# Score products of the latents' attention, issued sorted by the number of rows of their operands within a head pair

## The chip, the core and the metric

The kernel runs on one core of one Trainium2 chip. The metric is the device time of one execution in microseconds (us); lower is better. TensorE (PE in the profile) does the matrix products, VectorE (DVE) and ScalarE (ACT) the elementwise work, GpSimd (POOL) some of it, and SyncE (SP) issues the loads of weights.

## What is computed

The reference is two networks in a row on 512 tokens of width 1024. The first block mixes a gated delta rule with dilated attention and ends in a layer with product-key experts. The second block has two layers. Each mixes gated linear attention, neighborhood attention and sliding-window attention over 512 latents and 256 context tokens, and then runs a gated feed-forward network. The change touches the latents' neighborhood and window attention only, whose scores are

```python
# neighborhood attention, 6 heads of width 64: keys near each query, and the context's keys
s_loc = jnp.einsum('brnqhd,brnkchd->bhrnqkc', q_blk, k_blk).astype(jnp.float32) * scale + bias
s_ctx = jnp.einsum('brnqhd,blhd->bhrnql', q_blk, kc).astype(jnp.float32) * scale
# sliding window, 6 query heads on 2 key heads: 3 blocks of 128 keys, and the context's keys
s_loc = jnp.einsum('bnqhgd,bnkhd->bhgnqk', qb, kb).astype(jnp.float32) * scale
s_ctx = jnp.einsum('bnqhgd,blhd->bhgnql', qb, kc).astype(jnp.float32) * scale
```

each followed by a softmax over both parts and the product with the values.

## The kernel before

**Precision.** Every float32 operand of a large product is split into an upper part, rounded to the format that TensorE multiplies in one pass, and a lower part, the rest. A product is the sum of upper x upper, lower x upper and upper x lower. In the weight products that is three matmuls (lines 463, 465 and 474) of 128 rows each. In the attention a head has only 64 features, so two of the three parts fit into one matmul: the upper half of an operand's 128 rows holds one part and the lower half the other. One score product of a head is therefore a pair of matmuls: a *whole* one with operands of 128 rows (queries `nqd` or `sqs`, keys `nks`, `rks`, `skd` or `rskd`), and a *half* one with operands of 64 rows (`nql` with `nks` or `rks` in the neighborhood, `sqs` with `skl` or `rskl` in the window). The half one adds to the columns that the whole one has just written. The half matmuls of head 0 of a pair have their operands in rows 0 to 63, those of head 1 in rows 64 to 127.

**Items.** The attention's work is cut into items: one item is a pair of heads and one tile of 128 queries. A layer has 12 neighborhood items and 12 window items. `cuts[p]` lists for head p the pieces of columns of PSUM and the operands of the whole and the half matmul of each. Neighborhood items, and window items at both ends of the sequence, have 512 columns of scores per head. Head 0 fills one bank of PSUM and head 1 the next, in four pieces and eight matmuls. Window items in the middle of the sequence have 640 columns per head, so that the two heads meet within a bank: five pieces, ten matmuls, three banks. The keys are the moving operand (256 columns in most pieces), the queries the stationary one, loaded anew for each matmul.

**Order.** Each item is a small program per engine (`attend`). TensorE writes the scores and gives the semaphore marks "half" after head 0 and "scores" after head 1. VectorE (line 2308) reads them with the bias, finds the smallest value and stores them in SBUF (`NS`, `SS`). ScalarE (line 2274) takes the exponential, VectorE and ScalarE divide (lines 2331, 2334 and 2281), TensorE turns the weights (line 2247), ScalarE and VectorE copy them back (2287, 2340), TensorE multiplies with the values (line 2255, operands of 128 rows and 64 columns), and VectorE copies the result out (2344). A planner that runs when the kernel is built interleaves these items with weight products and puts all of it into one fixed order per engine. It counts the yields of each program and not its matmuls. Each engine then runs its own list in order, and only semaphores tie them.

The loop that issues the scores before the change is, for each head,

```python
for c0, c1, parts in it.cuts[p]:
    ...
    for k, (q, key) in enumerate(parts):
        ins = t.x.matmul(sp[:, c0:c1], q, key, start=k == 0, stop=k == len(parts) - 1)
```

Of the kernel before, what the change touches and what calls it, by code (L numbers as in the profile page):

```python
# [331 lines left out]
def program(nc, io):  # L332
# [52 lines left out]
    def hold(t, b, *by):  # L385
        for flag in freed.get(b, ()):
            t.wait_ge(*flag)
        freed[b] = by
        return bank[b]
# [1784 lines left out]
    def next_item(e, lane):  # L2174

        k = e.state[lane.name] = e.state.get(lane.name, -1) + 1
        if laying(e):
            left = lists[lane.m.name, lane.items]
            for j in (k, k + 1):
                if (lane.name, j) not in assigned:  # L2180
                    assigned[lane.name, j] = left.pop(0) if left else None
        return assigned[lane.name, k]

    def pick(t, lane, step, it):

        def left():
            return [g[:it.count] for g in lane.groups if not busy & set(g[:it.count])]
        if laying(t):
            while not left():
                yield Until(left)  # L2190
            group_of[step, it.key] = min(left(), key=lambda g: max(free_at.get(b, 0.0) for b in g))
# [17 lines left out]
    def attend(lane):  # L2209
        S, m = lane.S, lane.m  # L2210

        def tensor(t):
            while it := next_item(t, lane):
                n = it.n
                yield When(("operands", m.name, it.out))
                if out_event(it):
                    yield When(out_event(it))
                yield from pick(t, lane, "scores", it)
                for b in group_of["scores", it.key]:
                    hold(t, b, ("attend_v", it.key, "least", 1) if it.bias is not None else ("attend_a", it.key, "exp", 1))  # L2220
                note(t, "scores", it, it.count == 1, 3.5)
                sp = banks_of("scores", it)
                operands_tensor(t, it)
                shared = {c0 // 512 for c0, _, _ in it.cuts[0]}
                for p in range(2):
                    if p and it.count == 1:
                        yield 0.5
                    for c0, c1, parts in it.cuts[p]:
                        if p and c0 // 512 in shared:
                            t.wait_ge("attend_t", it.key, "half")  # L2230
                        for k, (q, key) in enumerate(parts):
                            ins = t.x.matmul(sp[:, c0:c1], q, key, start=k == 0, stop=k == len(parts) - 1)
                    ins.then_inc(*t.gives("attend_t", it.key, "scores" if p else "half"))
                note(t, "scores", it, False, 3.5)
                yield Mark(("swept", it.key))
                yield 4.0
                yield from pick(t, lane, "turn", it)
                note(t, "turn", it, True)
                sp = banks_of("turn", it)
                for b in group_of["turn", it.key]:  # L2240
                    hold(t, b, ("attend_v", it.key, "out"))
                for k in range(it.count):
                    t.wait_ge("attend_v", it.key, "weights")
                    if cells(it, k).stop > n:
                        t.wait_ge("attend_a", it.key, "weights")
                    for b in range(4 * k, cells(it, k).stop // 128):
                        ins = t.x.transpose(sp[:, 128 * b:128 * b + 128], S[:, 128 * b:128 * b + 128], ident)
                    ins.then_inc(*t.gives("attend_t", it.key, "turn", k))
                yield 1.0
                values_tensor(t, it)  # L2250
                for k in range(it.count):
                    t.wait_ge(*turned(it, k))
                for j in range(n // 128):
                    for p in range(2):
                        ins = t.x.matmul(sp[hs[p], 0:128], it.vals[p][j], S[:, n * p + 128 * j:n * p + 128 * j + 128],
                                         start=j == 0, stop=j == n // 128 - 1)
                ins.then_inc(*t.gives("attend_t", it.key, "out"))
                note(t, "turn", it, False, 0.6)
                if laying(t):
                    attended[it.m.name, it.out] = attended.get((it.m.name, it.out), 0) + 1  # L2260
                    if attended[it.m.name, it.out] == m.NT:
                        yield Mark(("attended", m.name, it.out))
                yield 0.2
# [128 lines left out]
    def out_event(it):  # L2392

        if not it.m.lat:
            return f"split {it.m.name} {it.out - 3}" if it.out >= 3 else None
        if it.out >= 4:
            return f"split {it.m.name} {it.out - 4}"
        return f"values {it.m.name} {it.out - 1}" if it.out else None
# [1588 lines left out]
```

## Time and profile before

| | |
|---|---|
| time, median of 3 runs | 4315.93 us (4309.71 to 4316.92) |
| time of the profiled execution | 4310.04 us |
| its span on the core | 4308.2 us |
| TensorE busy | 3970.9 us, 92% of the span |
| VectorE busy | 2391.3 us, 56% |
| ScalarE busy | 1690.4 us, 39% |
| mean granted clock of TensorE | 0.946 |

The span is the time from the core's first to its last instruction; 1.8 us of the execution lie outside it. A matmul's record has a start and a duration that includes the way through the array, so that records overlap; what a matmul costs in a row of others is the distance from its start to the next one's start. The granted clock is 1.0 at 2.4 GHz and 0.5 at 1.2 GHz.

### The profile page before, as it was taken

The numbers are of one execution on the slowest core, as the hardware profiler recorded it, in microseconds if no ns is written. First come the engines' busy times: TensorE is split into PE (matmuls) and PEld (weight loads), VectorE is DVE, ScalarE is ACT, GpSimd is POOL, SyncE is SP. The second block draws the span as 40 slices with busy tenths as digits, with TensorE's granted clock in tenths as the row PEclk, the third lists the DMA queues.
The fourth block names the chain that finished last, engine by engine and source line by source line (L and its number), as shares of the span: only waits on it lengthen the run. The fifth ranks groups of instructions, "written<-read, shape, count | busy, mean of one in ns | idle before, by whom it ended". The sixth has DMA issues, their size and how long they took to land. (4 is left out here: it accounts for less than half of the span.)

```text
span 4308.2 us, 57393 instructions
## 1 busy us (share of the span) xinstructions
PE 3970.9 (92%) x23037; PEld 3390.5 (79%) x23037; DVE 2391.3 (56%) x4212; ACT 1690.4 (39%) x2807; POOL 731.4 (17%) x580
## 2 busy tenths in 40 slices
PE   7899998988898779999999999888899998899998
PEld 4678876776798779999999998666688776567887
DVE  4444324455788758777777776545533345545333
ACT  3422333343356773333333334334432233444222
POOL 0012000252214423223222322000000010101000
PEclk8999999998998889999999999987899999869999
DMA  5311234432344458888888884211133431101322
GB/s 200 116 45 38 65 106 149 170 100 76 104 160 161 144 199 303 274 286 278 282 287 273 288 276 147 79 49 36 67 126 120 137 122 52 61 20 61 98 96 79
DMA packets 209193, 617.30 MB, mean 143 GB/s; under 512 B 18464, under 2 KB 68640, under 8 KB 205088
## 3 DMA queue, kind: packets, MB, share of 16 engines
q1 hardware_dynamic: 168352, 465.76, 33.2%
q0 software_dynamic: 40576, 147.87, 9.8%
q8 instruction: 183, 3.00, 0.3%
q14 instruction: 82, 0.67, 0.1%
HBM read 583.67 MB, written 29.88 MB: 142 GB/s over the span
## 5 line engine op out<-in xcount | busy, mean ns | idle before, releaser
L463 PE MATMUL ps<-hhi,whi 128*128 128x512 f32 (+1 forms) x2824 | 1100.1, 390 | 29.4 <-ACT whi L421 19.2
L429 DVE TENSOR_TENSOR wlo<-raw,whi 128x1024 fp32r<-128x1024 f32 x576 | 714.1, 1240 | 715.4 <-ACT whi L421 715.1
L465 PE MATMUL ps<-hlo,whi 128*128 128x512 f32 (+1 forms) x2824 | 1064.8, 377 | 0.3 <-DVE hlo L2440 0.2
L421 ACT ACTIVATE whi<-raw 128x1024 fp32r<-128x1024 f32 x660 | 694.1, 1053 | 664.3 <-PE ps L474 507.8
L474 PE MATMUL ps<-hhi,wlo 128*128 128x512 f32 (+1 forms) x2824 | 671.3, 376 | 0.0
L463 PEld LDWEIGHTS ps<-hhi,whi 128*128 128x128 f32 x2824 | 543.4, 192 | 135.6 <-issue 47.5
L465 PEld LDWEIGHTS ps<-hlo,whi 128*128 128x128 f32 x2824 | 543.7, 193 | 74.0 <-issue 7.2
L474 PEld LDWEIGHTS ps<-hhi,wlo 128*128 128x128 f32 x2824 | 514.7, 190 | 74.4 <-issue 5.7
L463 PE MATMUL ps<-ag_hi,whi 128*128 128x384 f32 x1024 | 342.2, 334 | 0.0
L465 PE MATMUL ps<-ag_lo,whi 128*128 128x384 f32 x1024 | 342.1, 334 | 0.0
L429 POOL TENSOR_TENSOR wlo<-raw,whi 128x1024 fp32r<-128x1024 f32 x85 | 206.4, 2436 | 322.5 <-ACT whi L421 322.1
L3310 POOL DMA_INDIRECT fetched<-peer_u_rows,rows x128 | 149.0, 1164 | 389.0 <-DVE ract L3268 344.5
L3310 POOL DMA_INDIRECT fetched<-peer_v_rows,rows x128 | 149.5, 1168 | 363.1 <-DVE xtok L3282 338.7
L3195 ACT ACTIVATE uact<-ps 128x384 f32<-128x384 f32 x128 | 62.9, 492 | 373.4 <-PE ps L474 373.4
L474 PE MATMUL ps<-ag_hi,wlo 128*128 128x384 f32 x1024 | 198.1, 334 | 0.0
L463 PE MATMUL ps<-hchi,whi 128*128 128x256 f32 x672 | 180.0, 301 | 17.1 <-ACT whi L421 8.1
L463 PEld LDWEIGHTS ps<-ag_hi,whi 128*128 128x128 f32 x1024 | 192.3, 188 | 0.0
L465 PEld LDWEIGHTS ps<-ag_lo,whi 128*128 128x128 f32 x1024 | 192.2, 188 | 0.0
L474 PEld LDWEIGHTS ps<-ag_hi,wlo 128*128 128x128 f32 x1024 | 179.3, 187 | 0.0
L465 PE MATMUL ps<-hclo,whi 128*128 128x256 f32 x672 | 173.3, 291 | 0.0
L3268 DVE CUSTOM_DVE_ANT_0 fetched<-fetched,xtok 128x1024 f32<-128x1024 f32 x128 | 156.0, 1219 | 12.3 <-DMA fetched<-peer_u_rows,rows 12.3
L3282 DVE SCALAR_TENSOR_TENSOR xtok<-fetched,ract,xtok 128x1024 f32<-128x1024 f32 x127 | 162.4, 1279 | 0.0
(629 smaller groups left out, 6189.9 us busy)
## 6 DMA issues: line engine op xcount, KB each, us to landing
raw<-w_in SPq DMA_DIRECT2D x151, 512.0 KB, 3.6
raw<-peer_u SPq DMA_DIRECT2D x128, 512.0 KB, 4.7
raw<-peer_v SPq DMA_DIRECT2D x128, 512.0 KB, 4.2
raw<-w_mod SPq DMA_DIRECT2D x96, 512.0 KB, 4.2
raw<-w_gate SPq DMA_DIRECT2D x66, 512.0 KB, 3.5
raw<-w_up SPq DMA_DIRECT2D x66, 512.0 KB, 3.5
raw<-w_down SPq DMA_DIRECT2D x66, 512.0 KB, 3.5
gate_dram<-stage SPq DMA_DIRECT2D x24, 1024.0 KB, 4.6
```

What stands on the lines that cost most here:

```text
L421: a.x.activation(whi[n % NW][:], raw[i % NRAW][:], ACT.Copy, bias=0.0, scale=1.0).then_inc(*a.gives("hi", i))
L429: e.x.tensor_tensor(wlo[n % NW][:], raw[i % NRAW][:], whi[n % NW][:].bitcast(F32), ALU.subtract).then_inc(*e.gives(*lo_sig(i)))
L463: t.x.matmul(o, w, p.hi, start=grp.opens and k == 0, stop=False)
L465: t.x.matmul(o, w, p.lo, start=False, stop=False)
L474: ins = t.x.matmul(o, lo[:, 128 * (starts[gi] + k):128 * (starts[gi] + k) + 128], p.hi, start=False, stop=grp.closes and k == len(grp.pair ...
L3195: a.x.activation(uact[j % 2][:], held(("out", "peer_u", j))[:, 0:TD], ACT.Gelu_apprx_tanh, bias=0.0, scale=1.0).then_inc(*a.gives("peer_a" ...
L3268: v.x.tensor_tensor_reduce(c[:], c[:], xtok[:], 1.0, 0.0, ALU.mult, ALU.add, ract[:, i:i + 1]).then_inc(*v.gives("expert_v", "dot", i))
L3282: v.x.scalar_tensor_tensor(xtok[:], c[:], ract[:, i:i + 1], xtok[:], ALU.mult, ALU.add).then_inc(*v.gives("expert_v", "sum", i))
L3310: g.x.indirect_dma_start(fetched[i % NF][:], None, io["peer_v_rows" if i >= 128 else "peer_u_rows"], bass.IndirectOffsetOnAxis(ap=rows[:, ...
```

## The change

Within each head of an item all whole matmuls are now issued first and then all half ones, and in head 1 of an item whose heads share no bank it is the other way round, so that the half ones of both heads stand together. `shared` is now the set of banks that both heads write; only matmuls into those wait for "half". In a bank that a head writes in several pieces, only the first matmul has `start` and only the last has `stop`. The context's own attention has one matmul per piece, and its order stays as it was.

```diff
-                shared = {c0 // 512 for c0, _, _ in it.cuts[0]}
+                shared = {c0 // 512 for c0, _, _ in it.cuts[0]} & {c0 // 512 for c0, _, _ in it.cuts[1]}
                 for p in range(2):
                     if p and it.count == 1:
                         yield 0.5
-                    for c0, c1, parts in it.cuts[p]:
-                        if p and c0 // 512 in shared:
+                    pieces = sorted(it.cuts[p], key=lambda x: x[0] // 512 in shared) if p else it.cuts[p]
+                    whole, halves = [[(c0, c1, *parts[k]) for c0, c1, parts in pieces if k < len(parts)] for k in range(2)]
+                    row = halves + whole if p and not shared else whole + halves
+                    banks = [c0 // 512 for c0, _, _, _ in row]
+                    for k, (c0, c1, q, key) in enumerate(row):
+                        if p and banks[k] in shared:
                             t.wait_ge("attend_t", it.key, "half")
-                        for k, (q, key) in enumerate(parts):
-                            ins = t.x.matmul(sp[:, c0:c1], q, key, start=k == 0, stop=k == len(parts) - 1)
+                        ins = t.x.matmul(sp[:, c0:c1], q, key, start=banks[k] not in banks[:k], stop=banks[k] not in banks[k + 1:])
                     ins.then_inc(*t.gives("attend_t", it.key, "scores" if p else "half"))
```

The score matmuls stand at line 2232 before and at line 2235 after the change. On VectorE, ScalarE, GpSimd and SyncE the order of the instructions is the same before and after; on TensorE nothing moves but the score matmuls within their items.

The first place is the first neighborhood item of the first layer on TensorE. Before the change its eight matmuls stand so (rows with `nqd` are whole ones, rows with `nql` half ones; the first four belong to head 0):

```order
L2232 MATMUL ps<-l_nks_386,l_nqd_384 128x256
L2232 MATMUL ps<-l_nks_386,l_nql_385 128x256
L2232 MATMUL ps<-l_rks_387,l_nqd_384 128x256
L2232 MATMUL ps<-l_rks_387,l_nql_385 128x256
L2232 MATMUL ps<-l_rks_387,l_nqd_384 128x256
L2232 MATMUL ps<-l_rks_387,l_nql_385 128x256
L2232 MATMUL ps<-l_nks_386,l_nqd_384 128x256
L2232 MATMUL ps<-l_nks_386,l_nql_385 128x256
```

After the change the same item reads as follows; the row marked x2 is the last half matmul of head 0 and the first one of head 1.

```order
L2235 MATMUL ps<-l_nks_386,l_nqd_384 128x256
L2235 MATMUL ps<-l_rks_387,l_nqd_384 128x256
L2235 MATMUL ps<-l_nks_386,l_nql_385 128x256
L2235 MATMUL ps<-l_rks_387,l_nql_385 128x256 x2
L2235 MATMUL ps<-l_nks_386,l_nql_385 128x256
L2235 MATMUL ps<-l_rks_387,l_nqd_384 128x256
L2235 MATMUL ps<-l_nks_386,l_nqd_384 128x256
```

Two whole matmuls now open the item, four half ones stand in its middle, and two whole ones close it.

The second place is a window item in the middle of the sequence, whose heads share a bank. Before the change its ten matmuls on TensorE alternate (rows with `skd` and `rskd` are whole ones, with `skl` and `rskl` half ones; the first six belong to head 0):

```order
L2232 MATMUL ps<-l_skd,l_sqs_398 128x128
L2232 MATMUL ps<-l_skl,l_sqs_398 128x128
L2232 MATMUL ps<-l_skd,l_sqs_398 128x256
L2232 MATMUL ps<-l_skl,l_sqs_398 128x256
L2232 MATMUL ps<-l_rskd,l_sqs_398 128x256
L2232 MATMUL ps<-l_rskl,l_sqs_398 128x256
L2232 MATMUL ps<-l_rskd,l_sqs_398 128x256
L2232 MATMUL ps<-l_rskl,l_sqs_398 128x256
L2232 MATMUL ps<-l_skd,l_sqs_398 128x384
L2232 MATMUL ps<-l_skl,l_sqs_398 128x384
```

After the change, on TensorE, the same item:

```order
L2235 MATMUL ps<-l_skd,l_sqs_398 128x128
L2235 MATMUL ps<-l_skd,l_sqs_398 128x256
L2235 MATMUL ps<-l_rskd,l_sqs_398 128x256
L2235 MATMUL ps<-l_skl,l_sqs_398 128x128
L2235 MATMUL ps<-l_skl,l_sqs_398 128x256
L2235 MATMUL ps<-l_rskl,l_sqs_398 128x256
L2235 MATMUL ps<-l_rskd,l_sqs_398 128x256
L2235 MATMUL ps<-l_skd,l_sqs_398 128x384
L2235 MATMUL ps<-l_rskl,l_sqs_398 128x256
L2235 MATMUL ps<-l_skl,l_sqs_398 128x384
```

Each head is now a group of whole matmuls and a group of half ones. The wait for "half" stands ahead of the matmul with 384 columns of `skd` in both orders; one matmul now lies between it and head 0's last one, where two did before.

## Rows read from the trace of the kernel before

**Rows 1.** The page: busy time by engine, and TensorE's granted clock in 40 slices.

```profile
PE 3970.9 (92%) x23037; PEld 3390.5 (79%) x23037; DVE 2391.3 (56%) x4212; ACT 1690.4 (39%) x2807; POOL 731.4 (17%) x580
...
PEclk8999999998998889999999999987899999869999
```

**Rows 2.** Windows: stretch, length, busy us by engine, granted clock, DMA share, GB/s.

```profile
2838.00:3086.00 248.00, 214.45 (x1044) 149.78 (x1044) 126.56 (x305) 112.06 (x221) 13.33 (x16) 0.78 0.11 35
```

**Rows 3.** Timeline of TensorE, a neighborhood item at full clock: start, us, instruction.

```profile
2922.26 0.38 PE L2232 MATMUL ps<-l_nks,l_nqd 128*128 128x256 f32 x1
...
2924.76 0.50 PE L474 MATMUL ps<-hhi,wlo 128*128 128x512 f32 x1
```

**Rows 4.** Timeline of TensorE, a neighborhood item at half clock, and what follows.

```profile
2958.65 0.58 PE L2232 MATMUL ps<-l_nks,l_nqd 128*128 128x256 f32 x1 [1.45 <-DVE l_o L2344]
...
2962.73 0.47 PE L2255 MATMUL ps<-l_NS,l_nvtok 128*64 128x128 f32 x1
```

**Rows 5.** Timeline of TensorE, weight products of 256 columns, full and half clock.

```profile
851.02 0.28 PE L463 MATMUL ps<-hchi,whi 128*128 128x256 f32 x1
851.14 0.28 PE L465 MATMUL ps<-hclo,whi 128*128 128x256 f32 x1
...
886.48 0.41 PE L463 MATMUL ps<-hchi,whi 128*128 128x256 f32 x1
886.69 0.41 PE L465 MATMUL ps<-hclo,whi 128*128 128x256 f32 x1
```

**Rows 6.** Timeline of TensorE, context scores of 64 rows between weight products.

```profile
987.26 0.40 PE L463 MATMUL ps<-hhi,whi 128*128 128x512 f32 x1
987.50 0.40 PE L465 MATMUL ps<-hlo,whi 128*128 128x512 f32 x1
987.82 1.56 PE L2232 MATMUL ps<-c_res,c_nq 64*128 64x256 f32 x6
989.31 0.51 PE L463 MATMUL ps<-hhi,whi 128*128 128x512 f32 x1
```

**Rows 7.** Windows of line 2232 alone (PE, PEld, granted clock, DMA), half-clock stretches.

```profile
2838.60:2862.30 23.70, 8.28 (x16) 4.58 (x16) 0.57 0.13 45
...
2951.20:3005.70 54.50, 30.65 (x60) 17.21 (x60) 0.50 0.00 1
...
3029.70:3050.10 20.40, 13.45 (x26) 7.42 (x26) 0.50 0.00 0
...
3657.80:3678.10 20.30, 6.60 (x13) 3.54 (x13) 0.58 0.15 52
...
3883.00:3896.60 13.60, 9.08 (x18) 5.19 (x18) 0.50 0.00 0
```

**Rows 8.** Timeline of TensorE, context scores of one item and of two items together.

```profile
1047.68 0.70 PE L2232 MATMUL ps<-c_res,c_sq 64*128 64x256 f32 x2
...
1050.45 0.70 PE L2232 MATMUL ps<-c_res,c_sq 64*128 64x256 f32 x4
```

**Rows 9.** Timeline of VectorE after the first layer's first item.

```profile
2843.84 0.69 DVE L2308 CUSTOM_DVE_ANT_0 l_NS<-ps,l_NB 128x512 f32<-128x512 f32 x1
...
2851.85 0.69 DVE L2066 TENSOR_TENSOR l_tmp<-ps,l_C 128x512 f32<-128x512 f32 x1 [5.55 <-ACT l_C L1983]
```

**Rows 10.** Timeline at the end of the first layer's window items, VectorE and TensorE.

```profile
3073.79 0.88 DVE L2308 CUSTOM_DVE_ANT_0 l_SS<-ps,l_swm,nsink 128x640 f32<-128x640 f32 x1
...
3077.57 0.73 DVE L2308 CUSTOM_DVE_ANT_0 l_SS<-ps,l_swm,nsink 128x512 f32<-128x512 f32 x1
...
3082.74 0.29 PE L2255 MATMUL ps<-l_SS,l_res 128*64 128x128 f32 x1 [2.38 <-ACT l_SS L2287]
```

**Rows 11.** Timeline of TensorE, a window item that waits for its banks.

```profile
3029.67 0.58 PE L2232 MATMUL ps<-l_skd,l_sqs 128*128 128x256 f32 x1 [1.79 <-DVE l_st L2308]
```

**Rows 12.** Windows, all engines: neighborhood items among weight products; five window items.

```profile
2903.00:2944.00 41.00, 41.00 (x241) 28.25 (x240) 20.82 (x54) 17.80 (x35) 6.21 (x7) 1.00 0.25 82
...
2981.00:3003.00 22.00, 22.00 (x45) 12.30 (x43) 10.51 (x37) 9.15 (x23) 0.00 (x0) 0.50 0.00 0
```

## The prediction

> **What bounds the kernel now.** I read the page first: TensorE is busy 92% of the span [rows 1], so what matters is what its time is made of. Its clock is high in most slices and dips deepest in two places, slices 27 to 29 and 35 to 36 of 108 us each, and that is where the latents' attention of the two layers lies. The window over the first of them shows 248 us with TensorE busy for 214, VectorE for 127 and ScalarE for 112, at a mean clock of 0.78 [rows 2]; the second layer's window reads the same to within 1 us. TensorE is the bound there too, but with 248 - 214 = 34 us of waits per layer, so a matmul saved does not always shorten the stretch.
>
> Then I read the timeline, by distances from start to start. At full clock the eight score matmuls of an item take from 2922.26 to 2924.76, which is 0.3125 us each for 256 columns [rows 3]. At half clock they take from 2958.65 to 2962.73, 0.51 us each [rows 4]. A weight product of the same 256 columns costs 0.12 us at full clock and 0.21 us (0.213 over a longer row) at half clock [rows 5]. Those also add one matmul after the other into the same columns, so that the accumulation is not what costs. What differs is that the score matmuls alternate between operands of 128 and of 64 rows. The context's scores, all of 64 rows, isolate it: six of them, with neighbours of 128 rows at the two ends only, take from 987.82 to 989.31, 0.25 us each and less than the 0.3125 of the alternation, while the weight product of 512 columns just before them takes 0.32 us instead of the 0.24 of the one before it [rows 6]. The cost sits at the switch between the two forms, not in the form.
>
> **The change, step by step.**
>
> *Price of a switch.* 0.3125 - 0.12 = 0.1925 us at full clock, 0.51 - 0.213 = 0.297 us at half clock [rows 3 to 5]. Each matmul pays one switch now, since each has a neighbour of the other form on both sides.
>
> *How many go.* An item of eight matmuls has eight switches (its last leads back to a form of 128 rows) and keeps two; one of ten has ten and keeps four. Both lose six, and 48 items in two layers lose 288 of 408.
>
> *At which clock.* The half-clock stretches of the first layer hold 16 + 60 + 26 = 102 of its 204 score matmuls; those of the second, five stretches of which the first and last are shown, hold 105 [rows 7]. So 207 of 408 are at half clock, and of the switches removed 146 at 0.297 = 43.4 us and 142 at 0.1925 = 27.3 us. Together 70.7 us of TensorE.
>
> *Half matmuls of two heads side by side.* In 36 of the items the last half matmul of head 0 (rows 0 to 63, first bank) is now followed by the first of head 1 (rows 64 to 127, next bank). Four context matmuls of two items, in other rows and banks, took the same 0.70 us as two [rows 8]: such neighbours run at once. That hides one matmul per item, 0.107 us at full and 0.213 at half clock (256 columns at 2.4 and 1.2 GHz, just under the distances in [rows 5]), 18 items of each: 5.8 us more. From below it could be nothing.
>
> *Switches that stay after all.* Four half-clock items are followed directly by products with the values, which are of a third form (128 rows, 64 columns) [rows 4]; there a closing whole matmul has to switch too. 4 x 0.3 = 1.2 us back.
>
> *The wait for "half".* In the 12 items of ten matmuls the wait now comes one matmul after head 0's last one. Its record lasts 0.58 us at half clock [rows 4], and by then only about 0.51 + 0.21 us have passed before the waiting matmul could start. What is behind it on TensorE is the rest of the item, and its weight load can't be made early. I take 0.12 us each, 1.5 us, between nothing and a whole record (12 x 0.58 = 7 us). The other waits are unchanged, and "half" comes earlier for VectorE in the other items.
>
> *What the gain is lost to.* TensorE's list is fixed, so the question at each wait is whether what it waits for moves with the scores. Mostly it does: before 3029.67 TensorE waits 1.79 us for VectorE's two reads of scores that TensorE has just finished [rows 11], and this pair shifts as a whole. In three places it doesn't.
> First, each layer's first item: VectorE starts its read at 2843.84 with no idle time before, being busy with other operands until then, and TensorE later waits for line 2066, which hangs on ScalarE's list [rows 9]. The item's whole saving, 6 x 0.297 + 0.21 = 2.0 us at half clock, is lost, twice: 3.8 us with the second one partly at full clock.
> Second, each layer's last two window items: VectorE takes one item every 3.8 us (3073.79 to 3077.57) without idle time, and TensorE waits 2.38 us for the end of this chain [rows 10]. In the first layer that swallows the saving of the last two items, 12 x 0.1925 + 0.11 = 2.4 us. In the second the two are at half clock and save 3.8 us; TensorE reaches the same place later there, and I take 2.4 us of them as lost.
> Third, the item at 3029.67 and its twin: VectorE is still in the softmax of the item before when the scores are ready, about 0.5 us each.
> Together 3.8 + 4.8 + 1.0 = 9.6 us. The DMAs are at 0.11 of their time here [rows 2] and don't matter. The order of the other engines is the same, so nothing else moves.
>
> *Sum.* 70.7 + 5.8 - 1.2 - 1.5 - 9.6 = 64.2 us. On top, what is left of each stretch should run somewhat more often at full clock, since the same columns come in less time: the last short dip of the first layer (3074 to 3077) may vanish, and the clock may return a little earlier behind the window items. I allow 3 us. The profiled execution took 4310.04 us; 4310.0 - 67 = 4243. It is at the low end of the runs of before (4309.7 to 4316.9), so I put the time at 4244.
>
> *A rule against the change.* Were weight loads not hidden between two matmuls on the same rows, grouping would pay a load at each of the junctions it makes. The weight products show no such thing: same rows each time, and 0.12 us for 256 columns [rows 5], against 0.107 for the columns alone.
> The Trainium skill, "TensorE: Matmul & The Clock Gate", section "The mechanism" of its part on packing small matmuls, says that a weight load overlaps running matmuls only when the row groups differ; in another section it also allows it for a load into the background weight buffer. By the first sentence alone, each of the 288 new junctions would cost 128 columns at 1.2 GHz, an estimate of 0.107 us or 31 us in all, and the time would be about 4275. The trace sides with the second.
>
> **The rivals.**
>
> *More of it is absorbed (0.10).* VectorE and ScalarE need about 3.8 us per window item [rows 10], and five such items stand in a row, 22 us of TensorE [rows 12]. If this chain sets the pace wherever items stand close, the saving of the roughly 20 window items near others shrinks from 1.8 to about 0.6 us each, 24 us less: 4268. Against it: VectorE is busy only 10.5 of those 22 us [rows 12], and banks are freed after its reads, which come ahead of the rest of the chain.
>
> *The clock comes back (0.14).* In [rows 12] TensorE's records cover all 22 us and the clock is still 0.50; at 2922 the same alternation, between weight products, runs at 1.0 [rows 3]. If the closer order brings the window items to full clock, the half-clock items cost 0.9 us less again (8 x 0.51 - 6 x 0.297 = 2.3 against 8 x 0.3125 - 6 x 0.1925 = 1.35), and the other matmuls of these stretches gain as well. With 207 of 408 matmuls that is 24 items, 23 us; for the rest, what the stretches of [rows 7] hold beside the scores, I put 12 us; VectorE's chain takes back about half of the 35: 4226.
>
> The skill's same page, section "What's actually happening", has the clock follow how busy TensorE is. By that rule the stretch in [rows 12] would already be at full clock if busy meant covered by records, so the trace asks for another measure, and the denser order can only help; it leans to this rival.
>
> *The switch isn't what costs (0.03).* If the 0.19 us came with each half matmul wherever it stands, the change would move nothing: 4311 to 4316. Against it stand the context's scores, half matmuls in form, at 0.25 us each with two switches among six [rows 6], and four of them in the time of two [rows 8].
>
> *Slower (0.02).* The neighborhood items at full clock stand among weight products; from 2903 to 2944 TensorE has no wait at all and the clock is 1.0 [rows 12]. If TensorE, done sooner, waited more and its clock fell to half there, these 41 us of work would take up to 41 us more in each layer: 4246 + 82 = 4328. It decides once more than 64 us are lost so. For it: the clock is already down where items stand without weight products between them. Against it: nothing but dead time is taken out, and what replaces it is the next matmul, not a wait.
>
> **How the numbers follow.** My forecast has 0.71, with a range of its own from 4230 to 4262: the unknown terms are the side-by-side term (0 to 5.8), the wait for "half" (0 to 7), the losses (5 to 20) and the clock (0 to 15). The range for 8 in 10 reaches partly to both neighbours: 4222 to 4266. A measurement of this kernel tells 0.2%, some 9 us, from no change. Faster by more than that: 0.71 + 0.10 + 0.14 and a small part of the switch rival's failure to be complete, 0.95. Within it 0.03, slower 0.02.
>
> **What the profile after would show.** Within an item at full clock two whole matmuls start about 0.12 us apart, and an item of eight takes about 1.25 us at full and 2.1 at half clock instead of 2.50 and 4.08; the last half matmul of head 0 and the first of head 1 start within some nanoseconds. The stretch from the first score to the last value product shrinks by about 32 us in each layer, and everything ahead of 2838 is unchanged. The wait at 3082.74 grows to nearly 5 us. I would be wrong in the switch's price if whole matmuls follow at 0.2 us or more, in the losses if TensorE's waits per layer grow by much more than 5 us, and in the clock if the stretch around the five window items is at 1.0.

## The result, and the profile after

| | before | after |
|---|---|---|
| time, median | 4316.43 us (4309.71 to 4321.0, 4 runs) | 4267.24 us (4263.78 to 4270.94, 4 runs) |
| profiled execution, span | 4310.04, 4308.2 us | 4268.82, 4267.0 us |
| TensorE busy | 3970.9 us | 3885.8 us |
| mean granted clock | 0.946 | 0.952 |

The changed kernel is faster: the ratio is 0.9889 with a 95% interval of 0.9876 to 0.9901, or 49 us. The forecast was 4244 with a range up to 4266; the measured median lies 1 us above that range. The direction was right, and the gain two thirds of what was expected.

The page of the changed kernel, busy time by engine and TensorE's clock in 40 slices, against [rows 1]:

```profile
PE 3885.8 (91%) x23037; PEld 3355.6 (79%) x23037; DVE 2390.1 (56%) x4212; ACT 1686.0 (40%) x2807; POOL 728.7 (17%) x580
...
PEclk8999999999999899999999999988899999879999
```

TensorE's busy time fell by 85 us, that of the other engines hardly. The span fell by 41, so about half of what TensorE saved did not reach it. The windows over the two layers' stretches of the changed kernel (stretch, length, busy us by engine, granted clock, DMA share, GB/s), against [rows 2]:

```profile
2843.00:3070.00 227.00, 176.86 (x1082) 135.47 (x1083) 126.27 (x307) 109.73 (x221) 13.30 (x16) 0.81 0.13 39
3637.00:3862.00 225.00, 174.42 (x1082) 134.32 (x1083) 125.63 (x305) 109.02 (x220) 13.29 (x16) 0.82 0.13 39
```

TensorE now stands idle for 50 of 227 us where it was idle for 34 of 248. The timeline of TensorE of the changed kernel, a neighborhood item at full clock, against [rows 3]:

```profile
2921.59 0.38 PE L2235 MATMUL ps<-l_nks,l_nqd 128*128 128x256 f32 x1
2921.81 0.28 PE L2235 MATMUL ps<-l_rks,l_nqd 128*128 128x256 f32 x1
2922.02 0.38 PE L2235 MATMUL ps<-l_nks,l_nql 64*128 64x256 f32 x1
2922.03 0.49 PE L2235 MATMUL ps<-l_rks,l_nql 64*128 64x256 f32 x2
2922.25 0.28 PE L2235 MATMUL ps<-l_nks,l_nql 64*128 64x256 f32 x1
2922.46 0.39 PE L2235 MATMUL ps<-l_rks,l_nqd 128*128 128x256 f32 x1
2922.68 0.28 PE L2235 MATMUL ps<-l_nks,l_nqd 128*128 128x256 f32 x1
2922.80 1.10 PE L474 MATMUL ps<-hhi,wlo 128*128 128x512 f32 x4
```

The eight matmuls take 2922.80 - 2921.59 = 1.21 us instead of 2.50. Read the distances of the closing group: from the last half matmul to the next whole one 2922.25 to 2922.46, 0.21 us; from this whole one to the next 0.22 us; from the last whole one to the weight product 0.12 us. So a switch costs 0.09 us ahead of it and 0.10 us behind it, 0.19 together, as the prediction had it in one piece. The four half matmuls start in two pairs: two at 2922.02 and 2922.03, two within 0.01 us of each other at 2922.25 (the row marked x2 holds the second of the first pair and the first of the second). Which of them make a pair shows in an item of the changed kernel in which both heads take the keys in the same order, so that its list has `l_skl`, `l_rskl` of head 0 and then `l_skl`, `l_rskl` of head 1:

```profile
3015.32 0.39 PE L2235 MATMUL ps<-l_skl,l_sqs 64*128 64x256 f32 x2
3015.55 0.28 PE L2235 MATMUL ps<-l_rskl,l_sqs 64*128 64x256 f32 x2
```

The two with `l_skl` start together and, 0.22 us later, the two with `l_rskl`. So each half matmul of head 0 runs beside its counterpart of head 1, and head 1's first one starts ahead of head 0's second, against the order of the list.

TensorE, an item at half clock, and the wait ahead of it, against [rows 4] and, for the wait, [rows 9]:

```profile
2858.45 0.58 PE L2235 MATMUL ps<-l_nks,l_nqd 128*128 128x256 f32 x1 [7.84 <-DVE l_tmp L2066]
...
2860.49 0.84 PE L2540 MATMUL ps<-cst,l_nvT 128*128 128x128 f32 x3
```

That is 2.04 us instead of 4.08. **Where the time went** follows from the distances between the starts of TensorE's matmuls, split at each layer's first window item (what stands in brackets in the timeline is the wait, the rest is work; the first start and the last value product bound the stretch):

| part | before: us, of them waits | after |
|---|---|---|
| layer 0, neighborhood part | 141.5, 25.0 | 128.5, 32.3 |
| layer 0, window part | 108.2, 7.2 | 97.2, 17.0 |
| layer 1, neighborhood part | 140.3, 26.0 | 127.2, 33.3 |
| layer 1, window part | 107.0, 4.8 | 97.0, 16.9 |
| sum | 497.0, 63.0 | 449.9, 99.5 |

Work fell from 434.0 to 350.4, by 83.6 us; the score matmuls alone fell from 166.9 to 83.1. Waits grew by 36.5, of them 21.9 in the window parts. Net 47.1 us. (The profiled span shows 41 and not 47 because this execution reached the first score at 2843.86 instead of 2839.38. The code ahead is the same, and the profiled executions of the experiments reach it between 2839.5 and 2845.1.)

**The waits in the window part.** TensorE of the changed kernel, some of its rows in the run of five window items that [rows 12] showed without a wait, and behind it:

```profile
2972.33 0.27 PE L2235 MATMUL ps<-l_skd,l_sqs 128*128 128x256 f32 x1
...
2978.42 0.50 PE L2235 MATMUL ps<-l_skd,l_sqs 128*128 128x128 f32 x2 [1.64 <-DVE l_st L2311]
...
2981.93 0.58 PE L2235 MATMUL ps<-l_skd,l_sqs 128*128 128x256 f32 x1 [0.69 <-DVE l_st L2311]
...
2989.12 1.31 PE L2250 MATMUL ps<-cst,l_SS 128*128 128x128 f32 x10 [1.16 <-DVE l_st L2311]
```

Three items, 26 matmuls, start between 2972.33 and 2976.49; then TensorE waits for VectorE's reads of scores, which free the banks. VectorE's timeline of the changed kernel shows why these reads are late:

```profile
2973.30 0.75 DVE L2311 CUSTOM_DVE_ANT_0 l_SS<-ps,l_swm,nsink 128x512 f32<-128x512 f32 x1
...
2974.76 0.16 DVE L2327 TENSOR_TENSOR l_st<-l_st,nsink 128x2 f32<-128x2 f32 x1
2975.81 0.16 DVE L2330 TENSOR_TENSOR l_st<-l_st 128x2 f32<-128x2 f32 x1 [0.88 <-ACT l_st L2282]
2976.01 0.17 DVE L2334 RECIPROCAL l_st<-l_st 128x1 f32<-128x1 f32 x1
2976.21 0.49 DVE L2337 TENSOR_SCALAR l_SS<-l_SS,l_st 128x512 f32<-128x512 f32 x1
2976.61 0.16 DVE L2334 RECIPROCAL l_st<-l_st 128x1 f32<-128x1 f32 x1
2976.68 0.87 DVE L2311 CUSTOM_DVE_ANT_0 l_SS<-ps,l_swm,nsink 128x640 f32<-128x640 f32 x1
...
2980.46 0.73 DVE L2311 CUSTOM_DVE_ANT_0 l_SS<-ps,l_swm,nsink 128x512 f32<-128x512 f32 x1
```

On VectorE's fixed list the read of the next item's scores stands behind the whole softmax of this one, with a wait of 0.88 us for ScalarE's exponentials in the middle. VectorE takes one item per 3.38 us (2973.30 to 2976.68) or 3.78 us (to 2980.46), in turn for 512 and 640 columns. TensorE's score matmuls now take 1.2 us for eight and 2.0 for ten at full clock (2.0 and 3.4 at half clock); with 4.08 us for eight it was the slower of the two in this run before (22 us for five items, 4.4 each). Now VectorE's list is.

**The waits in the neighborhood part.** In the first layer the wait of [rows 9]'s line 2066 grew from 5.07 to 7.84 us, another from 5.77 to 6.77, and three are new. The first of these, on ScalarE and on TensorE of the changed kernel:

```profile
2909.00 0.72 ACT L2284 ACTIVATE l_NS<-l_NS,l_st 128x512 f32<-128x512 f32 x1 [0.23 <-DVE l_st L2334]
2909.63 0.58 ACT L1776 ACTIVATE l_sq<-ps 128x512 f32<-128x512 f32 x1
```

```profile
2910.35 1.18 PE L2621 MATMUL ps<-l_sq,c 128*128 128x512 f32 x2 [1.53 <-ACT l_sq L1776]
2926.50 1.10 PE L2621 MATMUL ps<-l_sk,c 128*128 128x512 f32 x2 [1.50 <-ACT l_sk L1776]
2941.10 0.63 PE L2627 MATMUL ps<-cst,l_svT 128*128 128x128 f32 x4 [1.53 <-ACT l_svT L1776]
```

ScalarE copies the fresh projection `l_sq` out of PSUM only after the scaling that ends an item's softmax on its list. TensorE, whose scores between the projection and its next use got shorter, now comes 1.5 us too soon. The stretch that [rows 12] had without a wait and at 1.00 holds such waits now and is at 0.93, while the window items' run is at full clock at its start. Windows of the changed kernel:

```profile
2903.00:2944.00 41.00, 36.44 (x246) 27.81 (x242) 22.77 (x60) 19.53 (x41) 6.91 (x8) 0.93 0.27 87
...
2972.00:2977.00 5.00, 4.77 (x29) 3.29 (x27) 3.40 (x11) 2.23 (x7) 0.00 (x0) 1.00 0.00 0
```

### The profile page after: what moved, and what is told of

Its sections match the earlier page's. It is cut to its first block and busy times, and to the rows that moved or that the text cites. A ratio compares the mean times of both kernels' runs of the same rounds, so it can differ in the third digit from the quotient of the medians.

```text
span 4267.0 us, 57393 instructions
## 1 busy us (share of the span) xinstructions
PE 3885.8 (91%) x23037; PEld 3355.6 (79%) x23037; DVE 2390.1 (56%) x4212; ACT 1686.0 (40%) x2807; POOL 728.7 (17%) x580
## 5 line engine op out<-in xcount | busy, mean ns | idle before, releaser
L465 PEld LDWEIGHTS ps<-hlo,whi 128*128 128x128 f32 x2824 | 543.3, 192 | 73.8 <-issue 7.0
```

Source lines behind the costliest of these rows:

```text
L465: t.x.matmul(o, w, p.lo, start=False, stop=False)
```

## The experiments

Times are medians with the lowest and highest run. The kernel before was run with each group: 4314.72 us (4311.64 to 4322.63) with the first four, 4316.78 (4310.76 to 4324.96) with the next four, 4316.12 (4310.99 to 4322.34) with the three after these, and 4313.6 (4312.45 to 4319.25) with the last. A ratio is to that one. Parts, waits and work are counted as in the table above.

**1 and 2. One kind of item each.** The new order only where the condition holds, the old loop elsewhere; the second has `it.out >= 3`.

```diff
+                if it.out < 3:
                     shared = {c0 // 512 for c0, _, _ in it.cuts[0]} & {c0 // 512 for c0, _, _ in it.cuts[1]}
...
+                else:
+                    shared = {c0 // 512 for c0, _, _ in it.cuts[0]}
...
```

Expected of the neighborhood items alone:

> Only the 24 neighborhood items have the new order; the window items alternate as before. Theory A (the gain is the switches removed, less what TensorE then waits longer for VectorE and ScalarE): these items save 8 x 1.29 + 4 x 2.04 = 18.5 us of TensorE per layer, and the waits around them grow by 7.4 us per layer as in the trace of the changed kernel, so about 22 us in all: 4294 us. Rival B (what is lost is lost in the window items alone, whose softmax has the longer chain, and the neighborhood items keep all they save): 37 us, 4279 us.

Expected of the window items alone:

> Only the 24 window items have the new order. Theory A: about 23 us of TensorE per layer saved, a good part of it by the return of the full clock, and about 10 us per layer lost to longer waits: 26 us in all, 4290 us, and the two parts add up to the whole change. Rival B (above): about 12 us, 4304 us. If the parts add to clearly less or more than 49 us, one part's waits hang on the other's.

Measured: 4290.0 us (4284.46 to 4291.46), ratio 0.9934 [0.9917, 0.9950], and 4292.64 us (4290.84 to 4294.17), ratio 0.9944 [0.9928, 0.9961]. The gains, 24.7 and 22.1 us, add up to 46.8, the 49 of the whole within the spread of the runs. Both kinds lose part of their saving by themselves; neither eats the other's.

**3. Without the turn in head 1.**

```diff
-                    row = halves + whole if p and not shared else whole + halves
+                    row = whole + halves
```

> In head 1 of the 36 items of eight matmuls the whole matmuls come first as well, so that these items keep four switches and the half matmuls of the two heads are not neighbours. TensorE needs 2 x 0.19 to 0.3 us more for the switches and 0.11 to 0.21 more for the matmul that is no longer hidden, about 0.65 us per item or 23 us. Theory A: a little over half of it shows, since the waits shrink by the rest: 4280 us. Rival C (VectorE's and ScalarE's chains set the pace wherever items stand, so TensorE's speed no longer matters): within 3 us of the changed kernel, 4267 us. If all of it shows, 4290 us.

Measured: 4270.5 us (4269.49 to 4282.62), ratio 0.990 [0.988, 0.9921]. Of the three forecasts the one of rival C, 4267 within 3 us, came nearest; theory A's 4280 was missed. The items are slower as they should be. TensorE of this kernel, one of them at full clock:

```profile
2921.18 0.39 PE L2235 MATMUL ps<-l_nks,l_nqd 128*128 128x256 f32 x1
...
2922.70 0.28 PE L2235 MATMUL ps<-l_nks,l_nql 64*128 64x256 f32 x1
2922.90 0.50 PE L474 MATMUL ps<-hhi,wlo 128*128 128x512 f32 x1
```

Two more switches and no matmul hidden behind a neighbour: eight starts span 1.52 us (2922.70 - 2921.18), against 1.09 (2922.68 - 2921.59) in the changed kernel. To the product behind it the item takes 1.72 us, where it took 2.50 with the same eight matmuls and four switches more: 0.195 us a switch. Over both layers the score matmuls take 105.1 us instead of 83.1. Yet the stretches grow by only 2.5 us, since 17.1 us of waits go and 2.4 us of other work. A quarter of all that was gained in the scores (22 of 84 us) is worth little here: 3.3 us between the medians, with overlapping runs.

**4. One form only.** The order of before, but every half matmul multiplies the operands of the whole one.

```diff
                         for k, (q, key) in enumerate(parts):
+                            if it.m.lat:
+                                q, key = parts[0]
```

> The order of the kernel before, but each half matmul of the latents multiplies the whole matmul's operands of 128 rows a second time, so all score matmuls have one form and there is no switch at all; the scores are wrong by that. Theory A (a switch between forms costs 0.19 or 0.3 us): the matmuls follow at 0.12 and 0.21 us, an item of eight takes 1.0 us at full clock, less than the 1.21 of the changed kernel, and the time is near that kernel's, 4260 to 4267 us. Rival D (the cost belongs to two matmuls in turn on the same columns, or to the order of the keys): distances stay at 0.31 and 0.51 us and the time at 4316 us.

Measured: 4256.34 us (4250.3 to 4261.66), ratio 0.9856 [0.9837, 0.9874]. TensorE of this kernel, the first item, at half clock:

```profile
2845.07 0.76 PE L2234 MATMUL ps<-l_nks,l_nqd 128*128 128x256 f32 x2 [3.39 <-ACT l_nqd L2585]
2845.63 1.05 PE L2234 MATMUL ps<-l_rks,l_nqd 128*128 128x256 f32 x4
2846.49 0.63 PE L2234 MATMUL ps<-l_nks,l_nqd 128*128 128x256 f32 x2
2846.91 1.05 PE L1920 MATMUL ps<-l_tmp,c 128*128 128x512 f32 x1
```

Eight matmuls in 1.84 us, 0.23 each, with the order and the columns of before and as many weight loads; the time is a little under the forecast. So neither the order of the keys nor two matmuls in turn on the same columns costs anything. This run has no half matmuls at all, so it can't tell a price of the half form from a price of the switch; experiment 3 can, since it keeps all half matmuls and takes away switches. Together they leave the alternation of forms. This kernel has the shortest scores of all, 34.6 us per layer, and the most waits, 54.8.

**5 and 6. A shorter softmax, in the changed kernel and in the one before.** TensorE's list is untouched.

```diff
+                        thin = slice(it.half[0].start, it.half[0].start + 64) if it.m.lat and not isinstance(v.x, Blank) else it.half[0]
-                        v.x.tensor_scalar(S[:, it.half[0]], S[:, it.half[0]], lane.root[:, col[0]], None, ALU.mult).then_inc(
+                        v.x.tensor_scalar(S[:, thin], S[:, thin], lane.root[:, col[0]], None, ALU.mult).then_inc(
...
-                items.append(Item(m, 3 + i, n, w + 256, cuts, vals, bias, nsink[:, 6 * m.l + i:6 * m.l + i + 4:3]))
+                items.append(Item(m, 3 + i, n, w + 256, cuts, vals, bias))
```

(ScalarE's scaling of head 1 in the same way.) Expected of the changed kernel with it:

> The changed kernel with a shorter softmax on VectorE and ScalarE: the weights of both heads are scaled in 64 columns instead of 512 or 640, and the window items leave out the sink (two small operations of VectorE and one of ScalarE, with the wait between the engines); the output is wrong by that. TensorE's list is the same. Theory A: the waits that took 37 us of the change's gain hang on this chain, which gets shorter by about 0.4 us per neighborhood item and 1.5 us per window item, so this kernel gains much more from it than the kernel before does: 4267 - 25 = 4242 us or less. Rival E (the waits hang on something else, such as the loads of bias tables or the evacuation's own time): 4262 us or more.

Expected of the kernel before with it:

> The kernel before with the same shorter softmax. Theory A: TensorE, slower in its scores, mostly hides this chain, so little is gained except where it waits already (5 to 10 us): 4308 us, and the distance to the changed kernel with the short softmax is 60 us or more instead of 49. Rival E: both lose the same, and the distance stays at 49 us.

Measured: 4230.76 us (4228.12 to 4234.82), ratio 0.9799 [0.9783, 0.9815], and 4309.56 us (4306.04 to 4313.39), ratio 0.9985 [0.9975, 0.9994]. The same relief is worth 36 us after the change and 7 before it, and the distance between the two orders grows from 49 to 78.8 us. This is the test of the lost gain: most of it hangs on VectorE's and ScalarE's chain.

**7 and 8. Small matmuls later in the plan.** The planner is made to hold back the rotary products on a fresh projection (line 2621) and the transposes of line 2627 by 1.8 us after ScalarE's copy, and the first neighborhood item by 5 us.

```diff
+    def until(delay):
+        then = plan.now() + delay
+        return Until(lambda: plan.now() >= then)
...
                 yield When(("evac", place_of["proj", (m, *keys[x])], 0))
+                if laying(t):
+                    yield until(1.8)
...
+                if laying(t) and event[1] == "normed":
+                    yield until(5.0)
```

Expected of the changed kernel with it:

> The changed kernel with weight products moved ahead of places where TensorE waits: the planner holds the four small matmuls that read fresh projections of the window attention back by 1.8 us after their evacuation, and the second lane of the neighborhood items by 5 us. No work is added or taken. Theory A: the three waits of 1.53 us per layer and most of the one of 7.8 us are filled, up to 4.6 + 5 us per layer, less what the moved products leave open elsewhere: 4267 - 12 = 4255 us. Rival F (the waits only move on, since the chain on VectorE and ScalarE behind them ends no earlier): 4265 us or more.

Expected of the kernel before with it:

> The same holding back in the kernel before. Theory A: the 1.53 us waits don't exist there, only the one of 5 us before the second neighborhood item can be filled: 4316 - 6 = 4310 us. If it gains as much as the changed kernel does, the waits filled there are not those that the change made.

Measured: 4258.72 us (4256.61 to 4259.91), ratio 0.9862 [0.9845, 0.9878], 8.5 us under the changed kernel. But also 4303.8 us (4301.27 to 4306.04), ratio 0.997 [0.9958, 0.9983], 13 us under the kernel before. The theory's expectation for the second was missed: holding these matmuls back fills waits that the old order had as well. So this version is an improvement of its own, and not evidence of where the gain went.

**9 and 10. The shorter softmax in one kind of item each**, in the changed kernel. The edit is that of 5 with a condition more on `thin`, `it.out < 3` or (shown) `it.out >= 3`; the sink is left out in the second only.

```diff
-                        thin = slice(it.half[0].start, it.half[0].start + 64) if it.m.lat and not isinstance(v.x, Blank) else it.half[0]
+                        thin = slice(it.half[0].start, it.half[0].start + 64) if it.m.lat and it.out >= 3 and not isinstance(v.x, Blank) else it.half[0]
```

Expected with the neighborhood items shortened:

> The changed kernel with a shorter softmax in the neighborhood items only: both engines scale 64 columns of the weights instead of 512 (the rest stays undivided, so the output isn't the reference's). The window items are untouched. With both kinds shortened the time was 4230.8, 36 us below the changed kernel. Theory A, the part of the gain that was lost sits in both kinds, since TensorE's three new waits of 1.5 us per layer stand in the neighborhood part and the grown ones in both: 4250, within 6 us. Rival G, it sits nearly all in the run of window items, where nothing else stands between them: this run stays above 4259.

Expected with the window items shortened:

> The changed kernel with a shorter softmax in the window items only: no sink, and the scaling in 64 columns (the output isn't the reference's). The neighborhood items are untouched. Theory A, the loss is shared: 4248, within 6 us. Rival G, it sits nearly all in the window items: below 4240. The two runs' savings should add up to the 36 us of both together, unless one feeds the other by the clock.

Measured: 4260.09 us (4258.57 to 4261.76), ratio 0.9874 [0.9857, 0.989], and 4237.55 us (4234.66 to 4240.89), ratio 0.982 [0.9804, 0.9836]. The gains of 7.1 and 29.7 us add up to the 36.5 of both. Here the rival is right: this chain limits the window items. VectorE of the second kernel:

```profile
2973.92 0.69 DVE L2314 CUSTOM_DVE_ANT_0 l_SS<-ps,l_swm 128x512 f32<-128x512 f32 x1
...
2976.29 0.80 DVE L2314 CUSTOM_DVE_ANT_0 l_SS<-ps,l_swm 128x640 f32<-128x640 f32 x1
```

An item takes 2.37 us where it took 3.38. Over 24 items that would be 24 us; in the two window parts the waits fell from 33.9 to 15.6 us. TensorE's work in them fell too, from 160.3 to 147.2, in the same list: with fewer waits it ran less at half clock, 30.6 us against 56.3.

In the neighborhood items theory A's 4250 was missed and 4260.09 is where the rival had it. Still the three new waits hang on this chain. ScalarE and TensorE of the first kernel:

```profile
2909.12 0.35 ACT L2285 ACTIVATE l_NS<-l_NS,l_st 128x64 f32<-128x64 f32 x1 [0.23 <-DVE l_st L2335]
...
2910.09 1.10 PE L2623 MATMUL ps<-l_sq,c 128*128 128x512 f32 x2 [1.15 <-ACT l_sq L1776]
```

The scaling ahead of the copy takes 0.35 us instead of 0.72, and the waits are 1.15, 1.14 and 1.15 us instead of 1.53, 1.50 and 1.53. But the wait of 7.34 us for VectorE's copy of the turned weights (line 2258) grew to 8.12. All waits of the two neighborhood parts fell only from 65.6 to 61.7 us, and most of the 7.1 us came as less work of TensorE.

**11. Only the rotary products later**, without the 5 us of the item (the two `until(1.8)` of 7 alone).

> One half of the version that was faster: the planner holds back the small matmuls on fresh projections by 1.8 us after ScalarE's copy, but doesn't hold back the first neighborhood item by 5 us. Theory A, in which the three new waits of 1.5 us per layer for ScalarE's copies are part of what ate the gain and this removes them: 3 x 1.5 x 2 = 9 us, so 4258, as the version with both had. Rival H, the 8.5 us came from the item that was put later: this run stays above 4263.

Measured: 4257.73 us (4254.72 to 4260.41), ratio 0.987 [0.9853, 0.9886]. The 5 us are worth nothing; the whole gain is in the rotary products. It is not quite as expected, though. On TensorE's timeline of this kernel no wait for the copies of `l_sq` and `l_sk` is left between 2895 and 2950, that for `l_svT` now stands ahead of an item, and one of 4.96 us has come, while that of 7.34 us at the products with the values is down to 1.88:

```profile
2924.93 0.39 PE L2239 MATMUL ps<-l_nks,l_nqd 128*128 128x256 f32 x1 [1.21 <-ACT l_svT L1776]
2933.74 1.97 PE L2254 MATMUL ps<-cst,l_NS 128*128 128x128 f32 x8 [4.96 <-DVE l_svtok L2659]
```

The first layer's neighborhood part has 29.0 us of waits, after 32.3, and the part is 3.9 us shorter.

**12. Both reciprocals ahead of the scaling**, in the window items, on top of 11.

```diff
                     v.x.reciprocal(lane.root[:, col[p]], lane.sums[:, col[p]]).then_inc(*v.gives("attend_v", it.key, "root", p))
-                    if p == 0:
+                    if p == (0 if it.sink is None else 1):
                         v.wait_ge("attend_v", it.key, "root", 0)
```

> The version with the later rotary products, and one thing more, in the window items only: VectorE takes both reciprocals before it scales head 0's weights (0.52 us), where it scaled between them, so that ScalarE can scale head 1's weights 0.5 us sooner. TensorE's list is the same as in the version without it; nothing is left out. Theory A, the time of the window items hangs on the chain through their softmax: with no sink and short scaling this chain was some 1.9 us per item shorter (0.16 + 0.19 + 0.16 on the sink, 0.45 and 0.7 in the scaling, and the hops between) and the time fell by 29.7 us; a quarter of that length is about a quarter of the gain, 7 us: 4251, within 4 us. Rival I, only large cuts in this chain reach TensorE since banks are freed by VectorE's reads ahead of it: 4256 to 4260.

Measured: 4250.14 us (4243.89 to 4251.84, 5 runs), ratio 0.9846 [0.9833, 0.986]. ScalarE's timeline of this kernel, the scaling of head 1 in the first window item:

```profile
2967.99 0.72 ACT L2288 ACTIVATE l_SS<-l_SS,l_st 128x512 f32<-128x512 f32 x1 [0.56 <-DVE l_st L2338]
```

VectorE's scaling of head 0 starts at 2967.93, so the two run side by side instead of one after the other. The two window parts take 184.4 us after 189.4. The intervals of 11 and 12 just meet, and they were timed in two sessions; that the second is faster rests on the medians (7.6 us) and on these parts. Why is less clear than the expectation had it: VectorE takes an item of 512 columns per 3.30 us and one of 640 per 3.72, after 3.38 and 3.77 in 11, which over 24 items is some 1.5 of these 5 us. It computes all of the reference and is the fastest such version here: 17 us under the changed kernel, 63.5 under the one before.

## Why the prediction was off

**The price of a switch: right.** 0.19 us at full clock and, at half clock, 0.30 (distances of 0.34 and 0.38 us around a switch against 0.21 without); items of 1.21 and 2.04 us where 1.25 and 2.1 were said. Experiments 3 and 4 together show that it is the alternation. The prediction's own ground for this was weaker than it said: of the six context matmuls of 64 rows in [rows 6], the middle ones, with no switch beside them, start 0.216 us apart and not 0.12. The average of 0.25 hid it, and why they take so long isn't shown. The latents' half matmuls don't: in the item of ten that starts at 2973.44 the middle one of three half ones takes 0.17 us, as the middle one of three whole ones does. The rule weighed against the change, a weight load that can't hide on the same rows, did not show: the two whole matmuls of `l_skd` and `l_rskd` at 2972.33 start 0.11 us apart.
The Trainium skill, "TensorEngine Tiling (Array Packing)", section "Key Properties", says that changing the tiling mode drains TensorE. The trace is in line with it, in that part of each switch is paid ahead of it (0.09 us) and part behind (0.10 us).

**Side by side: right in kind, too small in number.** The prediction had one matmul per item hidden, head 1's first behind head 0's last. Two are, since both half matmuls of head 1 start within 0.01 us of head 0's: the four take two distances (0.22 and 0.21 us) and not three. Within an item of eight the saving of 1.29 us (2.04 at half clock) is near the forecast of 1.26 (2.0) even so. Part of the sixth switch falls on the product behind the item, whose distance went from 0.34 to 0.23 us. Without the turn (experiment 3) the scores take 22.0 us more.

**The wait for "half": over-sized**, 1.5 us forecast and none seen: in the items of ten at half clock and at full clock the waiting matmul starts 0.38 and 0.22 us after the one before, as any first one after a switch does.

**The clock: under-sized in TensorE's work.** 73.8 us were forecast without it and 3 with it; the work fell by 83.6. Of the 408 score matmuls 118 are now at half clock, 204 before. Those 86 are nearly eleven items, and an item costs 0.83 us less at full clock: about 9 us, an estimate from these two figures.

**The step that failed is "What the gain is lost to".** It had 9.6 us in three kinds of places; the waits grew by 36.5. Two of its places were right: the first item (5.07 to 7.84 us; 2.0 were forecast) and the layer's end (2.38 us before; now 1.57, 2.20 and 1.30, which is the forecast of nearly 5). The third was not: the item at 3029.67 and its twin wait 1.79 us in both kernels, and it is the next item's wait that grew, from 0.85 to 2.14. Over both layers the waits of the first two places grew by 13.4 us, where 8.6 were forecast. The other 23 lie elsewhere, 11.5 of them in the run of five window items and just behind it. What it left out is that everything else on VectorE and ScalarE has a place in a list too. I looked for waits that exist and asked how they would grow. I did not ask at which speed of TensorE new ones arise. In the run of window items I set aside the rival that named this with two reasons. One was that VectorE is busy for only 10.5 of 22 us: but its list is held up by waits for ScalarE inside each softmax, so that it can be the bound at half its busy time. The other was that banks are freed by VectorE's reads, ahead of the rest of the chain: true within an item, but the read of the next item stands behind the rest of this one. The rows at hand said 3.8 us per item [rows 10], and my own 2.1 us for an item of eight at half clock, 1.25 at full, would have shown that TensorE outruns it. Experiments 5, 6 and 10 show it from VectorE's side, experiment 3 from TensorE's.
The Trainium skill, "TensorE: Matmul & The Clock Gate", section "Architectural detail: the array is 16× 32×32, not 1× 128×128", says that VectorE's and ScalarE's queues are strictly first in, first out. The rows agree: the read at 2976.68 starts 0.07 us after the start of the reciprocal before it, though the last matmul of its scores started at 2975.14 and lasted 0.33 us.

So the sum was 73.8 + 3 - 9.6 = 67; the runs show 83.6 - 36.5 = 47.1 in the stretches, and 49 in the time. The two misses point in opposite directions, 6.8 us too little work saved and 26.9 us too little waiting, so the total looks better than its terms. "More of it is absorbed" put 4268 and came nearest, with its mechanism; "the clock comes back" happened in part; how much of its 9 us reached the time isn't shown.

**What stays open.** Of the 14.6 us by which the waits of the neighborhood parts grew, experiment 9 shows for the three new ones per layer that they follow the length of ScalarE's softmax. The rest is read from the trace, and a shorter softmax there took only 3.9 us off these waits. The plan change of 7 and 11 gives back 8 to 10 us, but as much or more without the change in order (8), so it doesn't settle them one by one. How much of the 13 us of work that experiment 10 saved is the clock's, and how much of the clock is due to which wait, was not taken apart.

One correction to the text ahead of the prediction: the planner does put a price on matmuls by their columns when it interleaves the programs. What it doesn't know is the price of a switch between forms. Nothing in the prediction rests on it.

## What to carry to other kernels

Where matmuls of two operand shapes alternate, read the distance between starts and group them by shape. It costs nothing and gave 84 us of TensorE here. But when an engine gets faster in a stretch, first compute the pace of every other engine's list there, waits inside it included, and not its busy share: in the window items the gain ended where TensorE's time per item went under that pace. After that the next microsecond is in the other engine's order, as the exchange of two small instructions in experiment 12 suggests.

## What was not expected of the hardware

- A switch between operand forms is paid on both sides, about half of it on the matmul before and half on the one after (0.09 and 0.10 us at full clock, 0.13 and 0.17 at half clock).
- Half matmuls of two heads, in different rows and banks, don't start in the order of the list: head 1's first starts within 0.01 us of head 0's first, 0.22 us ahead of head 0's second (the rows at 3015.32 and 3015.55).
- How much of a stretch the records cover doesn't tell its clock. Before the change, 22 us with records all through ran at 0.50 [rows 12]. After it, 5 us of the same items with about as much of them covered (4.77 us) ran at 1.00, and the 41 us that had 1.00 are at 0.93, with waits of 1.5 us in them. So by one change one stretch gained clock and another lost it.
